# Stationary-weight units of a two-block transformer kernel: hi and lo steps paired tile by tile

## The chip, the cores and the metric

One Trainium2 chip, one core. The metric is the device time of one execution in microseconds (us). The engines are called as the profile calls them: PE (TensorE matmul), PEld (its weight loads), DVE (VectorE), ACT (ScalarE), POOL (GpSimd), SP (SyncE, which issues the weight DMAs).

## The reference, cut to what matters

The input is `x` of 256 tokens by 2048 features. It goes through two layers of a first block and one layer of a second block. Nearly all the work is dense projections of the form

```python
h = x @ w_in                      # 2048 x 6672, twice (first block)
mkv = mem @ w_mem_kv              # 2048 x 1024, twice
out = y @ w_out                   # 2048 x 2048, twice
proj = rms_norm(x) @ w_in_2       # 2048 x 11272
y_a @ w_up_a, y_b @ w_up_b        # 1024 x 2048 each
merged @ w_o                      # 2048 x 2048
h @ w_ffn_in                      # 2048 x 11264
(silu(gate) * up) @ w_ffn_down    # 5632 x 2048
```

all in fp32. Between them stand attention over bands, gated linear recurrences, memory attention, norms and gates, which are small.

## The kernel before, in words

**Precision.** Each fp32 operand is held as two fp32r numbers: hi (the rounded value) and lo (what is left of it). A product is three terms: hi times hi, hi times lo and lo times hi. `Split` (L117) keeps an activation as hi and lo side by side, so that `act.both(k)` is 512 columns (256 tokens of hi, 256 of lo) of feature tile k, and `act.hi_of(k)` the 256 hi columns alone.

**Units.** The weights come in units of 512 KB (128 partitions by 1024 columns). `plan` (L248) lists them in the order of use. For a unit, `send` (L291) issues the DMA on SP into one of NR = 5 `raw` buffers; `split` (L304) lets ACT write `wh` (a copy of `raw` rounded to fp32r) and then DVE write `wl` = `raw` - `wh`, in one of NH = 4 pairs of buffers. `cut[n]` is the pair of tokens (ACT's, DVE's) of unit n. When DVE has done unit n, SP may refill its `raw` buffer (`send(n + NR)`).

`take` (L373) gives the number of the next unit and writes the split of the unit AHEAD = 2 later into the queues of ACT and DVE. The pairs of buffers go round: `give_back` (L286) puts a pair at the end of the list `places` with the PE tokens that release it, one for `wh` and one for `wl`, and `split` takes the first of the list. So the split of unit n + 2, queued when unit n is taken, uses the pair of unit n - 2. Each engine works through its own queue in the order in which the Python program wrote it; semaphores tie them.

**Two kinds of units.**

- F units (`unit_f`, L419) give a transposed result (features by tokens). The weights are stationary: four feature tiles kk by two column tiles t. For each of these eight 128 x 128 tiles there is a hi step, whose weights are a tile of `wh` and whose moving operand is `act.both(k)` (512 columns, written to one PSUM bank), and a lo step, whose weights are the same tile of `wl` and whose moving operand is `act.hi_of(k)` (256 columns, added to columns 256 to 511 of the same bank). Tile t goes to bank `pr[t]`, so that the bank changes from one tile to the next. A step is one LDWEIGHTS and one MATMUL.
- T units (`token_steps`, L432, used in `cols_t`, `half_pass` and the last stage) have the activations stationary and 512 columns of `wh` or `wl` moving: 12 steps of 512 columns each.

`run_unit` (L403) writes first all hi steps, the first of them behind the ACT token of the unit (and other waits of the pass), then all lo steps, the first behind the DVE token. The last hi step and the last lo step each give a token, and these release `wh` and `wl`. In an F unit that is eight hi steps and then eight lo steps.

A pass (`cols_f`, L438) has two halves of four F units each (two for the 1024-row matrices); after a half, its two banks are read out by ACT and DVE (`join`, L587: ACT copies columns 256 to 511, DVE adds columns 0 to 255). Attention, recurrences, gates and norms are generators, of which a piece is written into the queues after each unit (`step_all`, `step_lane`).

The change touches `unit_f` alone. `run_unit` stays in use for T units.

Of the kernel before, what the change touches and what calls it, by code (L numbers as in the profile page):

```python
# [5 lines left out]
D, S, P = 2048, 256, 128  # L6
# [143 lines left out]
def build(nc, A, out):  # L150
# [3 lines left out]
    with ctx:  # L154
# [20 lines left out]
        def op(eng, fn, *waits):  # L175

            count[eng] += 1
            queues[eng].append((waits, fn(LATER), done[eng], 1))
            return (done[eng], count[eng])

        def mm(fn, *waits):

            queues["pe"].append((waits, fn(LATER), None, 0))
# [89 lines left out]
        sent, cut, t_const = [], [], []  # L273
# [12 lines left out]
        def give_back(n, hi_tok, lo_tok):  # L286

            if not (state["leave"] and any(place[n] is x for x in extra)):
                places.append((place[n], (hi_tok, cut[n][1]), (lo_tok,)))
# [83 lines left out]
        def take(ahead=None):  # L373

            n = state["next"]
            state["next"] += 1
            if state["ramp"]:
                state["ramp"] -= 1
                state["ahead"] += 1
            while len(cut) < min(n + (state["ahead"] if ahead is None else ahead) + 1, len(units)):  # L380
                split(len(cut))
            return n
# [15 lines left out]
        def one(fn, last, waits=()):  # L398
            if last:
                return op("pe", fn, *waits)  # L400
            mm(fn, *waits)

        def run_unit(n, hi_steps, lo_steps, waits, keep=False):  # L403


            toks = []
            for steps, w in ((hi_steps, cut[n][:1] + waits), (lo_steps, cut[n][1:])):
                for j, fn in enumerate(steps):
                    tok = one(fn, j == len(steps) - 1, w)
                    w = ()  # L410
                toks.append(tok)
            if not keep:
                give_back(n, *toks)
            return tok

        def step(o, s, m, start, stop):
            return lambda e: e.matmul(o, s, m, start=start, stop=stop, skip_group_check=True)

        def unit_f(act, pr, u, nu, waits):  # L419

            n = take()
            h, l = place[n]
            his, los = [], []
            for kk in range(4):
                k = 4 * u + kk
                for t in range(2):
                    o, c = banks[pr[t]], kk * S + t * P
                    his.append(step(o, h[:, c:c + P], act.both(k), k == 0, False))
                    los.append(step(o[:, S:2 * S], l[:, c:c + P], act.hi_of(k), False, k == 4 * nu - 1))
            return run_unit(n, his, los, waits)  # L430

        def token_steps(act, b, t, k, h, l, kk, start, stop):  # L432

# [24 lines left out]
        def cols_t(act, nk=KT, waits=(), first=0, tiles=None, pr=None, among=False, late=False):  # L458


            pr = pr or pair()
            ready = tuple(waits) + bank_free[pr[0]] + bank_free[pr[1]]
            for k0 in range(0, nk - 8 if late else nk, 2):
                if among and (k0 % 4 == 0 or among == "early" and k0 == 2):
                    among_tok.append(cut[take()])
                    ready += among_tok[-1]
                n = take()
                h, l = place[n]
                k_ = (k0 + first) % nk
                w = ready  # L470
                if tiles is not None and k_ % 4 == 0:
                    while tiles[k_ // 4] is None:
                        step_posts()
                    w += tiles[k_ // 4]
                ready = ()
                his, los = [], []
                for kk in range(2):
                    for t in range(2):
                        a, b = token_steps(act, banks[pr[t]], t, k_ + kk, h, l, kk, k0 + kk == 0, k0 + kk == nk - 1)
                        his += a  # L480
                        los += b
                tok = run_unit(n, his, los, w)
                if k0 + 2 < nk:
                    step_all()
                step_lane(0)
                step_lane(1)
            if not late:
                return pr, tok
            return pr, [take(), take(), take(0), take(0)]
# [15 lines left out]
        def cols_t_halves(made, hooks, between):  # L505


            pr = pair()
            ns = [take(0) for _ in range(4)]
            free = [bank_free[pr[t]] for t in range(2)]  # L510
            half_pass(X, pr, 0, ns, 0, True, False, True, [made[0, u // 2] + (free[0] if u == 0 else ()) for u in range(4)], hooks)
            state["ahead"], state["leave"] = AHEAD, True
            between()
            half_pass(X, pr, 1, ns, 0, True, False, False, [made[1, u // 2] + (free[1] if u == 0 else ()) for u in range(4)])
            for u in range(4, 8):
                n = take()
                his, los = [], []
                for kk in range(2):
                    for t in range(2):
                        a, b = token_steps(X, banks[pr[t]], t, 2 * u + kk, *place[n], kk, False, u == 7 and kk == 1)  # L520
                        his += a
                        los += b
                tok = run_unit(n, his, los, made[0, u // 2] + made[1, u // 2])
                step_all()
                step_lane(0)
                step_lane(1)
            state["leave"] = False
            return pr, tok
# [20 lines left out]
        def narrow_f(act, waits=()):  # L549


            pr = pair()
            n = take()
            w = cut[n] + tuple(waits) + bank_free[pr[0]]
            for k in range(KT):
                fn = lambda e: e.matmul(banks[pr[0]][0:48, :], place[n][0][:, 48 * k:48 * k + 48], act.both(k),
                                        start=k == 0, stop=k == KT - 1, skip_group_check=True)
                if k == KT - 1:
                    tok = op("pe", fn)
                else:  # L560
                    mm(fn, *w)
                w = ()
            give_back(n, tok, tok)
            return pr[0], tok
# [508 lines left out]
        for l_ in range(2):  # L1073
# [13 lines left out]
            b, tok = narrow_f(X, waits=x_ready)  # L1087
# [3 lines left out]
            def gate_sums():  # L1091
# [27 lines left out]
            pr, tok = cols_t(X)  # L1119
# [12 lines left out]
                lambda t, h, m=mv[l_]: m[:, t * 512 + h * P:t * 512 + (h + 1) * P],  # L1132
                y_tiles(yraw, 12), lambda t: S, m_ready, sm_bufs, outs, scale=SC))

            for g in range(2):
# [6 lines left out]
                pr, tok = cols_t(X)  # L1142
# [45 lines left out]
            for n in range(4):  # L1188
# [12 lines left out]
                pr, tok = cols_t(Y, first=8, tiles=tiles if n == 0 else None, among=l_ == 0 and n == 3, late=late)  # L1201
# [225 lines left out]
        for g in range(2):  # L1427
# [29 lines left out]
            if g:  # L1457
                pr, tok = cols_t(X)
# [7 lines left out]
            if g == 0:  # L1466
# [3 lines left out]
                lambda t, h, v_=v_: v_[:, t * 512 + h * P:t * 512 + (h + 1) * P], False, 1.0,  # L1470
                HNW, EPS_RMS, yraw2[:, 4 * g * S:4 * (g + 1) * S], ready, li_bufs, outs))
            if g == 0:
# [4 lines left out]
                b, tok = narrow_f(X)  # L1477
# [57 lines left out]
        for g in range(2):  # L1535
# [8 lines left out]
            pr, tok = cols_t(X)  # L1544
# [113 lines left out]
        for n in range(4):  # L1658
# [3 lines left out]
            pr, tok = cols_t(X, tiles=tiles3 if n == 0 else None, pr=pr, late=n == 3)  # L1662
# [125 lines left out]
        def ready_group(g):  # L1788
# [6 lines left out]
        pr, tok = cols_t_halves(feat.made, {  # L1795
            1: lambda: feat.turn(0, (2, 3), (6, 7), z0[2]), 2: lambda: feat.turn(1, (0, 1), (4, 5), z1[0]),
            3: lambda: feat.turn(1, (2, 3), spare, z1[1])}, between4)
# [5 lines left out]
        pr, tok = cols_t(X)  # L1803
# [36 lines left out]
        def down(k, c, n, w):  # L1840

            his, los = [], []
            for t in range(2):
                for b in range(2):
                    x, y = down_steps(k, c, t, b, n)
                    his += x
                    los += y
            return run_unit(n, his, los, w)

        for k in range(FF // P):  # L1850
# [3 lines left out]
            for c in range(2):  # L1854
                n = take()
                tok = down(k, c, n, ring[g] + ready[c])
# [8 lines left out]
        for t in range(2):  # L1865
            for c in range(2):
                for b in range(2):
                    steps = []
# [4 lines left out]
                    for i, fn in enumerate(steps):  # L1873
                        tok = one(fn, i == len(steps) - 1, w)
# [126 lines left out]
```

How the kernel before makes its waits and increments, by code:

```python
        def run(name, e):  # L1915
            seen = {}
            for waits, fn, s_, n in queues[name]:
                for s, v in waits:
                    if seen.get(s.name, 0) < v:
                        e.wait_ge(s, v)
                        seen[s.name] = v
                if fn is not None:
                    ins = fn(e)
                    if s_ is not None:
                        ins.then_inc(s_, n)
```

## Time and profile before

| | |
|---|---|
| three runs | 2424.87, 2426.34, 2426.42 us; median 2426.34 |
| the profiled execution: its own time | 2426.7 us |
| its span, from the first to the last instruction | 2424.9 us |
| PE busy | 2401.3 us (99%), 13053 matmuls |
| PEld busy | 2070.0 us (85%), 13053 loads |
| DVE busy | 1542.0 us (64%) |
| ACT busy | 1279.9 us (53%) |
| HBM traffic | 188 GB/s over the span |
| mean granted TensorE clock | 0.997 |

PE is busy when any matmul is under way. Matmuls overlap, since one lasts longer than the time to the next one's start, so a busy PE is not one that streams columns all the time. How long a step takes is read from the starts of successive steps. Columns of a timeline row are: start in us, duration in us from the first start to the last end of the merged instructions, engine, line, operation, output<-inputs by the program's names, tile and shape, and xN for N instructions merged; in brackets the idle time before it and what ended that. A LDWEIGHTS row reads `banks<-xx,wh` as its matmul does; line 83 is the helper that writes every matmul.

### The profile page before, as it was taken

Reading aid. Unit: us, or ns where it says so; the run is one execution under the profiler, and the core shown is the slowest. Engines: PE = TensorE matmul, PEld = TensorE weight load, DVE = VectorE, ACT = ScalarE, POOL = GpSimd, SP = SyncE. Lnnn points to the kernel's source line nnn. Section 1 sums busy time; section 2 is a strip of 40 time slices with the busy share of each in tenths; the row PEclk is TensorE's granted clock in tenths of the full one; section 3 lists DMA queues with packets and bytes.
Section 4 is the critical chain, followed back from the end, with each engine's and each line's share of the span. In section 5 each row is a group of like instructions: output and inputs, shape, how many; then the busy total and the mean of one; then the engine's idle time right before and its main releaser. Section 6 shows DMA issues by size and latency. Waiting matters only on the chain.

```text
span 2424.9 us, 32948 instructions
## 1 busy us (share of the span) xinstructions
PE 2401.3 (99%) x13053; PEld 2070.0 (85%) x13053; DVE 1542.0 (64%) x1755; ACT 1279.9 (53%) x1738; POOL 7.5 (0%) x14
## 2 busy tenths in 40 slices
PE   9999999999999999999999999999999999999998
PEld 7888888888888888788888888888888888888887
DVE  6575567665655677685765567766566666665555
ACT  5445466444445655565664457554655555554443
POOL 0000000000000000000000000000000000000000
PEclk9999999999999999999999999999999999999999
DMA  8544546665445664544445545575555555557553
GB/s 297 195 156 148 182 164 262 216 222 181 149 150 181 235 235 144 186 162 151 165 157 182 174 156 175 191 275 188 187 197 186 182 191 193 182 191 254 195 191 139
DMA packets 127850, 458.84 MB, mean 189 GB/s; under 512 B 13616, under 2 KB 20304, under 8 KB 124752
## 3 DMA queue, kind: packets, MB, share of 16 engines
q1 hardware_dynamic: 126736, 450.38, 53.6%
q0 software_dynamic: 816, 6.29, 0.7%
q8 instruction: 102, 1.67, 0.3%
q14 instruction: 52, 0.43, 0.1%
q10 hardware_dynamic: 144, 0.07, 0.0%
HBM read 448.30 MB, written 8.39 MB: 188 GB/s over the span
## 4 chain that ended last, share of the span: by engine, by line
PE 94%; DVE 2%; ACT 2%; DMA 1%; issue 1%; DVEq 0%; SPq 0%; ACTq 0%
PE banks L83 93%; PE banks L86 1%; ACT wh L47 1%; DVE wl L50 1%; DMA raw<-in_w_in_f 0%; ACT tb L47 0%; DMA raw<-in_kv_t 0%; DVE x_buf L59 0%; ACT sm_s L47 0%; ACT t L47 0%; DVE b L62 0%; DVE o_buf L50 0%; DVE sm_s L50 0%; DVE u L50 0%; DVE ub L50 0%
## 5 line engine op out<-in xcount | busy, mean ns | idle before, releaser
L50 DVE TENSOR_TENSOR wl<-raw,wh 128x1024 fp32r<-128x1024 f32 x776 | 937.1, 1222 | 391.1 <-ACT wh L47 389.4
L47 ACT ACTIVATE wh<-raw 128x1024 fp32r<-128x1024 f32 (+1 forms) x779 | 803.2, 1051 | 347.7 <-PE banks L83 241.0
L83 PE MATMUL banks<-xx,wh 128*128 128x512 f32 (+1 forms) x3760 | 948.8, 394 | 0.0
L83 PEld LDWEIGHTS banks<-xx,wh 128*128 128x128 f32 (+1 forms) x3760 | 674.9, 188 | 128.0 <-issue 0.7
L83 PEld LDWEIGHTS banks<-xx,wl 128*128 128x128 f32 x3712 | 506.3, 190 | 36.7
L83 PE MATMUL banks<-xx,wl 128*128 128x256 f32 x3712 | 517.4, 282 | 0.0
L83 PE MATMUL banks<-wh,xx 128*128 128x512 f32 x1504 | 376.3, 390 | 0.0
L83 PEld LDWEIGHTS banks<-wh,xx 128*128 128x128 f32 x1504 | 280.6, 188 | 57.7
L83 PE MATMUL banks<-wl,xx 128*128 128x512 f32 x752 | 203.9, 389 | 0.0
L83 PEld LDWEIGHTS banks<-wl,xx 128*128 128x128 f32 x752 | 141.2, 188 | 29.3
L83 PE MATMUL banks<-wh,yy 128*128 128x512 f32 x416 | 103.5, 390 | 1.6 <-ACT wh L47 1.6
L83 PEld LDWEIGHTS banks<-wh,yy 128*128 128x128 f32 x416 | 77.7, 188 | 18.4 <-ACT wh L47 2.4
L47 ACT ACTIVATE le<-le 128x512 f32<-128x512 f32 (+1 forms) x32 | 27.1, 846 | 90.8 <-DVE le L50 84.6
L83 PE MATMUL banks<-yy,wh 128*128 128x512 f32 x256 | 64.1, 392 | 0.0
L47 ACT ACTIVATE hraw<-banks 128x512 f32<-128x512 f32 x20 | 12.0, 598 | 87.2 <-PE banks L83 87.2
L47 ACT ACTIVATE z<-banks 128x512 f32<-128x512 f32 x24 | 14.3, 598 | 78.9 <-PE banks L83 78.9
L83 PE MATMUL banks<-wl,yy 128*128 128x512 f32 x208 | 55.9, 389 | 0.0
L50 DVE TENSOR_TENSOR hraw<-banks,hraw 128x512 f32<-128x512 f32 x20 | 13.8, 692 | 64.7 <-ACT hraw L47 64.7
L83 PEld LDWEIGHTS banks<-yy,wh 128*128 128x128 f32 x256 | 46.0, 189 | 8.2
L50 DVE TENSOR_TENSOR xl<-raw,xh 128x1024 fp32r<-128x1024 f32 x32 | 38.6, 1223 | 20.7 <-ACT xh L47 20.4
L47 ACT ACTIVATE xh<-raw 128x1024 fp32r<-128x1024 f32 x32 | 33.3, 1058 | 30.6 <-PE banks L83 16.8
L50 DVE TENSOR_TENSOR z<-banks,z 128x512 f32<-128x512 f32 x24 | 16.6, 691 | 51.4 <-ACT z L47 51.4
(234 smaller groups left out, 1881.2 us busy)
## 6 DMA issues: line engine op xcount, KB each, us to landing
raw<-in_w_in_f SPq DMA_DIRECT2D x304, 512.0 KB, 3.3
raw<-in_w_ffn_f SPq DMA_DIRECT2D x160, 512.0 KB, 3.6
raw<-in_w_ffn_down SPq DMA_DIRECT2D x88, 512.0 KB, 4.3
raw<-in_w_in_t SPq DMA_DIRECT2D x80, 512.0 KB, 3.5
raw<-in_w_out_t SPq DMA_DIRECT2D x64, 512.0 KB, 5.0
raw<-in_w_o_t SPq DMA_DIRECT2D x32, 512.0 KB, 4.5
raw<-in_kv_t SPq DMA_DIRECT2D x16, 512.0 KB, 5.3
raw<-in_kv_f SPq DMA_DIRECT2D x16, 512.0 KB, 4.2
```

The lines of the kernel that those rows point to most:

```text
L47: return lambda e: e.activation(*a, **k)
L50: return lambda e: e.tensor_tensor(*a, **k)
L83: return lambda e: e.matmul(*a, **k)
L86: return lambda e: e.transpose(*a, **k)
```

## The change

For each of the eight tiles of an F unit, the hi step is followed at once by the lo step on the same tile; then comes the next tile. The first step of the unit waits for both tokens of `cut[n]` (ACT's for `wh` and DVE's for `wl`). Only the last step of the unit gives a token, and this one token releases both `wh` and `wl`.

```diff
@@ -420,14 +420,17 @@ (unit_f)
             n = take()
             h, l = place[n]
-            his, los = [], []
+            steps = []
             for kk in range(4):
                 k = 4 * u + kk
                 for t in range(2):
                     o, c = banks[pr[t]], kk * S + t * P
-                    his.append(step(o, h[:, c:c + P], act.both(k), k == 0, False))
-                    los.append(step(o[:, S:2 * S], l[:, c:c + P], act.hi_of(k), False, k == 4 * nu - 1))
-            return run_unit(n, his, los, waits)
+                    steps.append(step(o, h[:, c:c + P], act.both(k), k == 0, False))
+                    steps.append(step(o[:, S:2 * S], l[:, c:c + P], act.hi_of(k), False, k == 4 * nu - 1))
+            for j, fn in enumerate(steps):
+                tok = one(fn, j == len(steps) - 1, cut[n] + waits if j == 0 else ())
+            give_back(n, tok, tok)
+            return tok
```

The number of steps, their operands, their sizes and the order of units stay as they are.

## Rows read from the trace of the kernel before

**Rows 1.** Busy time by engine, and the chain that ended last by engine (page).
```profile
PE 2401.3 (99%) x13053; PEld 2070.0 (85%) x13053; DVE 1542.0 (64%) x1755; ACT 1279.9 (53%) x1738; POOL 7.5 (0%) x14
...
PE 94%; DVE 2%; ACT 2%; DMA 1%; issue 1%; DVEq 0%; SPq 0%; ACTq 0%
```

**Rows 2.** PE's steps by kind, with counts (groups by form).
```profile
L83 PE MATMUL banks<-xx,wl 128*128 128x256 f32 x3712 | 517.4, 282 | 0.0
L83 PE MATMUL banks<-yy,wl 128*128 128x256 f32 x256 | 35.7, 282 | 0.0
L83 PE MATMUL banks<-mem,wl 128*128 128x256 f32 x128 | 17.8, 282 | 0.0
```

**Rows 3.** Timeline, PE: the start of an F unit, and of the 45th after it.
```profile
1465.34 2.00 PE L83 MATMUL banks<-xx,wh 128*128 128x512 f32 x8
...
1591.04 1.32 PE L83 MATMUL banks<-yy,wh 128*128 128x512 f32 x5
```

**Rows 4.** Timeline, PE: F units following one another.
```profile
1802.60 2.00 PE L83 MATMUL banks<-xx,wh 128*128 128x512 f32 x8
1804.44 1.11 PE L83 MATMUL banks<-xx,wl 128*128 128x256 f32 x8
1805.39 2.00 PE L83 MATMUL banks<-xx,wh 128*128 128x512 f32 x8
```

**Rows 5.** Timeline, PEld: single loads around the two switches of those units.
```profile
1801.65 0.19 PEld L83 LDWEIGHTS banks<-xx,wl 128*128 128x128 f32 x1
1801.76 0.19 PEld L83 LDWEIGHTS banks<-xx,wl 128*128 128x128 f32 x1
...
1802.60 0.19 PEld L83 LDWEIGHTS banks<-xx,wh 128*128 128x128 f32 x1
1802.83 0.19 PEld L83 LDWEIGHTS banks<-xx,wh 128*128 128x128 f32 x1
1803.07 0.19 PEld L83 LDWEIGHTS banks<-xx,wh 128*128 128x128 f32 x1
...
1803.76 0.19 PEld L83 LDWEIGHTS banks<-xx,wh 128*128 128x128 f32 x1
...
1808.18 0.19 PEld L83 LDWEIGHTS banks<-xx,wh 128*128 128x128 f32 x1
1808.42 0.19 PEld L83 LDWEIGHTS banks<-xx,wh 128*128 128x128 f32 x1
```

**Rows 6.** Timeline, PE: the F unit behind a run of T steps.
```profile
102.83 1.98 PE L83 MATMUL banks<-xx,wh 128*128 128x512 f32 x8
104.64 1.12 PE L83 MATMUL banks<-xx,wl 128*128 128x256 f32 x8
```

**Rows 7.** Timeline, PEld: two 256-column matmuls onto the same columns of a bank.
```profile
1438.59 0.19 PEld L83 LDWEIGHTS banks<-negative,ident_r 128*128 128x128 f32 x1
1438.71 0.19 PEld L83 LDWEIGHTS banks<-xx,wh 128*128 128x128 f32 x1
```

**Rows 8.** Waits of PE, the largest group (releaser: us in total, times, longest).
```profile
PE banks L83 <- DVE lqe L50: 7.3, 3, 5.2
```

**Rows 9.** Timeline, DVE and PE: a lo split that ends after its unit began.
```profile
33.22 1.23 DVE L50 TENSOR_TENSOR wl<-raw,wh 128x1024 fp32r<-128x1024 f32 x1 [0.89 <-ACT wh L47]
34.21 2.00 PE L83 MATMUL banks<-mem,wh 128*128 128x512 f32 x8
...
1005.92 1.22 DVE L50 TENSOR_TENSOR wl<-raw,wh 128x1024 fp32r<-128x1024 f32 x1
1006.23 2.00 PE L83 MATMUL banks<-xx,wh 128*128 128x512 f32 x8
```

**Rows 10.** Timeline, PE: behind the last such unit.
```profile
1029.28 2.04 PE L83 MATMUL banks<-lqe,lke 128*128 128x128 f32 x8 [5.25 <-DVE lqe L50]
```

**Rows 11.** Timeline, PE and ACT: a release of `wh` and the split that follows.
```profile
2045.62 2.00 PE L83 MATMUL banks<-xx,wh 128*128 128x512 f32 x8
2047.70 1.06 ACT L47 ACTIVATE wh<-raw 128x1024 fp32r<-128x1024 f32 x1 [1.24 <-issue]
```

## The prediction

> **What bounds the kernel now.** I read the chain of work that ended last first: 94% of it is PE [rows 1]. PE is busy for 2401.3 of 2424.9 us, so that all its gaps together are 23.6 us [rows 1], and the largest group of its waits, for `lqe`, has 7.3 us in three waits [rows 8]. So the kernel ends when PE has gone through its steps, and what counts is the time from one step's start to the next. The groups by form give the number of steps with lo weights, one for each pair that the change reorders: 3712 + 256 + 128 = 4096, in 512 F units of eight pairs [rows 2].
>
> The price of a pair today: between two starts of F units 45 apart lie 1591.04 - 1465.34 = 125.70 us [rows 3], 2.793 us a unit, 349.1 ns a pair. Inside a unit the eight hi steps take 1.84 us (1802.60 to 1804.44), 230 ns each, and the eight lo steps 0.95 us, 119 ns each [rows 4]. 4096 pairs at 349.1 ns are 1430 us, 59% of the span. So one nanosecond per pair is worth 4.1 us. The whole question is whether a hi and a lo step side by side cost more or less than 349.1 ns.
>
> Single weight loads say what a step costs by its place [rows 5]. A load starts as the matmul before it starts, so their distances are those of the steps. Among the lo steps, the first after hi steps takes 0.11 us (1801.65 to 1801.76), and the other seven 0.84 together (1801.76 to 1802.60), 120 ns each; with 0.953 for all eight (2.793 less 1.84) the first has 113 ns. Among the hi steps, the first takes 0.23 (1802.60 to 1802.83; 0.24 in another unit, from 1808.18), the second 0.24, and the first five 1.16 together, 232 ns each; the last three of a unit are left with 1804.44 - 1803.76 = 0.68, 227 ns each [rows 4, 5]. A unit that comes behind 512-column steps of a T run has its eight hi steps in 104.64 - 102.83 = 1.81 us, 226 ns each [rows 6], where eight take 1.84 behind lo steps. So a settled hi step costs 227 ns, and after lo steps it takes about five hi steps, some 27 ns in all, to settle. The first lo step is cheap (113 ns), each lo step behind a lo step costs 120.
>
> **The change, part by part.**
>
> *The order of steps.* Nothing is added or removed on PE: 16 loads and 16 matmuls a unit before and after. Every lo step becomes a first lo step, and every hi step a first hi step. The trace never has the two kinds in turn, so the price must be bounded. A lo step lies between 113 ns (the first after hi) and 120 (in a run); it is nearest to the first kind, since a 512-column step stands ahead of it: 113. A hi step lies between 227 (settled) and 236 (the second after a switch, where the row's 0.24 is read at its lower side); it is nearest to the first hi step behind a lo step, 0.23 to 0.24: 233.3. The pair is 346.6 to 346.7 ns, 2.4 less than today. 4096 x 2.4 ns = 9.8 us. The two ends are 227 + 113 = 340 (-37 us) and 236 + 120 = 356 (+28 us).
>
> *What of it reaches the end.* Of the chain 94% is PE [rows 1]. Where PE waits for another engine, what it saves ahead of the wait is lost. I take 9.8 x 0.94 = 9.2 us.
>
> *The bank.* The lo step adds to the columns that the hi step ahead of it has just written, where today the bank alternates from step to step. The nearest row: two 256-column matmuls that add to the same columns of one bank, 0.12 us apart, the price of any lo step [rows 7]. In the change the distance at those columns is the same, since the hi step writes them in its second half. Cost nothing; if it isn't so, it shows as a pair above 349 ns, like the third rival.
>
> *The wait at the unit's start.* Today lo weights may be ready 1.84 us after the start. DVE finishes the lo split of most units well ahead. In six units it ends after the unit has begun, for instance at 33.22 + 1.23 = 34.45 against 34.21, and at 1005.92 + 1.22 = 1007.14 against 1006.23 [rows 9]. The other overshoots are of the same size or smaller, and the six sum to 2.7 us. Four of the six lie between 1006 and 1021 us, ahead of the idle 5.25 us in which PE waits for the chain of DVE that makes `lqe` [rows 10], and vanish in it. The two at 34 and 45 us cost 0.24 and 0.21 us and some 0.1 us each for the load that waits with them. Queued behind the waiting step are the unit's other steps and nothing of other work. I take +0.6 us; the bound is 0 below and 3 above.
>
> *The later release of `wh`.* The token of the last hi step, 0.95 us ahead of the unit's end, goes. ACT does use it: the hi steps of the unit at 2045.62 end at 2047.62, and the next split starts at 2047.70 [rows 11]. It will start about 0.9 us later. That split is for the unit four further on, which starts at 2045.62 + 4 x 2.79 = 2056.8. Split and lo split take 1.06 + 1.23 us and would end at about 2051, with 6 us to spare. What ACT has queued behind the split are pieces of attention and gates that depend on PE work behind later units, and the DMA that refills `raw`, also 0.9 us later, has over four units. Cost nothing; with the cover gone (where ACT and DVE are the chain, 4% of it [rows 1]) at most 0.9 us at each of three waits for `lqe` [rows 8], +3 us. One token less per unit on PE: nothing to be seen.
>
> *Sum.* The profiled execution took 2426.7 us, its span is 2424.9. 2426.7 - 9.2 + 0.6 = 2418.1. The median of the runs is 0.4 below the profiled one, so 2417.7; I say 2418.
>
> **The rivals.** About 0.2% (5 us) is what a measurement of this kernel can tell from no change.
>
> *Settled pairs: 2392 us.* The five slow hi steps may be a matter of leaving a run of lo steps, and with hi and lo in turn PE may never leave its settled state. Then the pair is 340 ns: 9.1 x 4096 = 37 us, 35 of them on the chain, +0.6. For it: each load has a longer step to hide beside half of the time, and 113 and 227 are exactly in the ratio of the columns. Against it: it is the lo steps that put the hi steps out of their settled state, and in the change every hi step stands behind one.
>
> *No difference: 2427 us.* The cheap first lo step may be borrowed from the hi steps, and given back. If the alternation stays unsettled, a hi step costs 232 or 233 and a lo step 116 to 117: 349. For it: the first lo step is 7 ns cheaper than the others, and the first hi step 6 dearer than a settled one, which nearly cancels. A page would put it here by another way. The Trainium skill, "TensorE: Matmul & The Clock Gate", sections "LDWEIGHTS (loading the stationary operand)" and "Back-to-back issue gap", gives a load of 128 columns 107 ns and a warm step its columns over 2.4 GHz plus 2.5 ns, 216 and 109; the load then fits beside either step, so the order would not matter. The trace doesn't agree on the size (227 and 113 to 120).
>
> *The load beside the short step: 2443 us.* Each hi tile's weights can only be loaded while the 256-column lo step runs. If a lo step between two hi steps is held by that load as those of a run are, it costs 120 ns, and the hi step behind it 233: 353.3 ns, +4.2 x 4096 x 0.94 = +16.2, +0.6. It decides for slower from about 350.3 ns a pair on. For it: today's last lo step, behind which a hi tile is loaded, takes 0.12 as well. Against it: the first lo step after hi takes 0.11 although the load beside it is as long. With 236 for the hi step it would be 2454.
>
> **How the numbers follow.** Forecast (a gain between 5 and 20 us) 0.42; settled 0.14; no difference 0.22; load beside the short step 0.22, half of it above 2434. The prediction is 2418. The range reaches down over the settled case (2390) and up over no difference with the 3 us waits and the lower half of the slower case (2434). Faster by over 0.2%: 0.42 + 0.14 = 0.56. Within 0.2%: 0.22. Slower: 0.22.
>
> **What would show it.** In the profile after: PE rows of 16 steps no longer in eights; starts of F units 2.77 us apart in place of 2.793 (2.72 in the settled case, 2.83 in the slower one); loads alternately 0.23 and 0.11 apart; T units unchanged at 227 ns a step; the waits for `lqe` within 1 us of before; a first-step wait for `wl` near 34 and 45 us of a few tenths. I am wrong if the unit's period moves by less than 0.01 us or upward, or if PE's waits grow by more than 3 us.

## The result, and the profile after

The changed kernel takes 2434.59 us (median of 6 runs, 2433.78 to 2435.97) against 2425.99 for the kernel before on the same chip; the ratio is 1.0038, 95% interval [1.0025, 1.0051]. It is 8.6 us slower. The forecast was 8 us faster, and the measured time lies just above the range.

The page of the changed kernel, engines and the chain that ended last, which answer to [rows 1]:

```profile
PE 2408.4 (99%) x13053; PEld 2059.8 (85%) x13053; DVE 1543.5 (63%) x1755; ACT 1286.6 (53%) x1738; POOL 7.5 (0%) x14
...
PE 93%; DVE 3%; ACT 2%; DMA 1%; issue 1%; SPq 0%; DVEq 0%; ACTq 0%
```

The same number of steps on PE, the same chain. The span grew from 2424.9 to 2434.2 us. Two terms can carry that: the steps and the waits. Waits first, to [rows 8] (releaser: us in total, times, longest):

```profile
PE banks L83 <- ACT wh L47: 5.9, 8, 1.2
PE banks L83 <- DVE lqe L50: 5.8, 3, 4.0
PE banks L83 <- DVE wl L50: 1.3, 3, 0.9
```

The wait for `wl` is new (1.3 us), the one for `lqe` is 1.5 us shorter, the one for `wh` has grown. That is not 9 us. The steps: the timeline of PE in the ffn stage, where the starts of successive rows are the starts of successive steps, answers to [rows 4, 5]:

```profile
1800.11 0.40 PE L83 MATMUL banks<-xx,wh 128*128 128x512 f32 x1
1800.34 0.28 PE L83 MATMUL banks<-xx,wl 128*128 128x256 f32 x1
1800.46 0.40 PE L83 MATMUL banks<-xx,wh 128*128 128x512 f32 x1
1800.69 0.28 PE L83 MATMUL banks<-xx,wl 128*128 128x256 f32 x1
1800.81 0.40 PE L83 MATMUL banks<-xx,wh 128*128 128x512 f32 x1
1801.05 0.28 PE L83 MATMUL banks<-xx,wl 128*128 128x256 f32 x1
1801.17 0.40 PE L83 MATMUL banks<-xx,wh 128*128 128x512 f32 x1
```

From 1800.11 to 1801.17 are three pairs in 1.06 us: 353 ns a pair, the hi steps 0.23, 0.23 and 0.24, the lo steps 0.12, 0.12 and 0.12. Another stretch of the same kernel, the merge of the two mixers:

```profile
1519.90 0.39 PE L83 MATMUL banks<-yy,wh 128*128 128x512 f32 x1
1520.13 0.27 PE L83 MATMUL banks<-yy,wl 128*128 128x256 f32 x1
1520.24 0.40 PE L83 MATMUL banks<-yy,wh 128*128 128x512 f32 x1
1520.47 0.28 PE L83 MATMUL banks<-yy,wl 128*128 128x256 f32 x1
1520.59 0.39 PE L83 MATMUL banks<-yy,wh 128*128 128x512 f32 x1
1520.82 0.27 PE L83 MATMUL banks<-yy,wl 128*128 128x256 f32 x1
1520.93 0.40 PE L83 MATMUL banks<-yy,wh 128*128 128x512 f32 x1
```

Here three pairs take 1.03 us. Over longer stretches, between a unit's start and that of the 45th unit after it in the merge stage, and of the 154th in the ffn stage:

```profile
1469.98 0.39 PE L83 MATMUL banks<-xx,wh 128*128 128x512 f32 x1
...
1594.78 0.39 PE L83 MATMUL banks<-yy,wh 128*128 128x512 f32 x1
...
1747.81 0.40 PE L83 MATMUL banks<-xx,wh 128*128 128x512 f32 x1
...
2183.11 0.40 PE L83 MATMUL banks<-xx,wh 128*128 128x512 f32 x1
```

124.80 / 45 = 2.773 us a unit, 346.7 ns a pair, and 435.30 / 154 = 2.827 us, 353.3 ns. The kernel before had 2.793 in both [rows 3, 4]. So the new order has two rhythms, one cheaper and one dearer than eight and eight. Taking the steps of each unit behind its first eight, every one of the 512 F units is clearly in one of the two: 199 at 346.7, 313 at 353.3. In 411 places one such unit follows another with nothing between them; the rhythm changes in one of them, behind a stop of PE of 0.94 us (at 1011.89). In steps that is 313 x 8 x 4.2 ns - 199 x 8 x 2.4 ns = +6.7 us.

The two traces, summed from start to start, give the same: all steps that read `wh` or `wl` as weights take 1450.6 us before and 1457.3 after. The stops of PE (the time beyond a step's usual distance) cost 3.1 us more: 0.65 at the two starts that wait for `wl` near 33 and 45 us, 3.3 at waits of T units for `wh` near 395 and 865 us, less 0.8 elsewhere. The other steps take 0.8 us less. In the profiled execution before, the granted clock was 0.69 from 10 to 14 us, behind PE stops of 1.1 and 2.0 us: seven T steps there lie 427 ns apart in place of 227 (some 1.5 us), which the changed kernel's trace hasn't. Together with 0.2 us at the end this makes up the 9.3 us between the two spans.

### The profile page after: what moved, and what is told of

It is laid out like the page before. It is cut to its first block, busy times and chain, and to the rows that moved or that the text cites. A ratio compares the mean times of both kernels' runs of the same rounds, so it can differ in the third digit from the quotient of the medians.

```text
span 2434.2 us, 33355 instructions
## 1 busy us (share of the span) xinstructions
PE 2408.4 (99%) x13053; PEld 2059.8 (85%) x13053; DVE 1543.5 (63%) x1755; ACT 1286.6 (53%) x1738; POOL 7.5 (0%) x14
## 4 chain that ended last, share of the span: by engine, by line
PE 93%; DVE 3%; ACT 2%; DMA 1%; issue 1%; SPq 0%; DVEq 0%; ACTq 0%
PE banks L83 92%; PE banks L86 1%; DVE wl L50 1%; ACT wh L47 1%; DMA raw<-in_w_in_f 1%; ACT tb L47 0%; DMA raw<-in_kv_t 0%; ACT t L47 0%; DVE x_buf L59 0%; ACT sm_s L47 0%; DVE b L62 0%; DVE ub L50 0%; DVE o_buf L50 0%; DVE le L50 0%; DVE sm_s L50 0%
## 5 line engine op out<-in xcount | busy, mean ns | idle before, releaser
L83 PE MATMUL banks<-xx,wh 128*128 128x512 f32 (+1 forms) x3760 | 1326.5, 399 | 0.9 <-DVE wl L50 0.9
L83 PE MATMUL banks<-xx,wl 128*128 128x256 f32 x3712 | 1039.1, 280 | 0.0
L83 PEld LDWEIGHTS banks<-xx,wh 128*128 128x128 f32 (+1 forms) x3760 | 703.2, 187 | 173.9 <-ACT t L47 1.2
L83 PEld LDWEIGHTS banks<-xx,wl 128*128 128x128 f32 x3712 | 700.8, 189 | 0.8
L83 PE MATMUL banks<-wh,xx 128*128 128x512 f32 x1504 | 376.4, 390 | 0.0
L83 PE MATMUL banks<-yy,wh 128*128 128x512 f32 x256 | 88.8, 394 | 0.0
L83 PE MATMUL banks<-yy,wl 128*128 128x256 f32 x256 | 70.9, 277 | 0.0
```

Source lines behind the costliest of these rows:

```text
L83: return lambda e: e.matmul(*a, **k)
```

## The experiments

The theories: **A**, the order of long and short steps costs, and waits do little; **B**, the joint wait and the late release cost; **C**, the lo step is held by the bank that the hi step ahead of it writes; **D**, a rhythm is caught where PE enters a run of pairs, and kept; **E**, the stage sets the rhythm by its traffic or addresses. Ratios are to the kernel before, run on the same chip in turn.

### Eight and eight with the new waits

```diff
-            return run_unit(n, his, los, waits)
+            steps = his + los
+            for j, fn in enumerate(steps):
+                tok = one(fn, j == 15, cut[n] + waits if j == 0 else ())
+            give_back(n, tok, tok)
+            return tok
```

> The steps stay eight hi and eight lo; the unit waits for both splits at its start and gives one token at its end, as in the changed kernel. Theory A (the order of the steps costs, the waits and the later release do little): units stay 2.793 us apart, and the time is 1 to 2.5 us above the kernel before, with PE's waits up by that much (near 34, 45, 385 and 940 us). Theory B (the later release and the joint wait are what costs): the time is 7 to 9 us above the kernel before.

2428.05 us against 2425.68: +2.4, ratio 1.0012 [1.0003, 1.0021], which is 0.7 to 5.1 us. The waits are a real term, at the upper end of theory A's sum, and by the medians less than a third of the loss. B, which asked for 7 to 9 us, falls as the main cause.

### Pairs with the release and the lo wait of before

The first step waits for `cut[n][:1]`, the second for `cut[n][1:]`; steps 15 and 16 give a token each.

> Hi and lo in turn as in the changed kernel, but the first lo step alone waits for the lo split, and the last hi step gives the token that releases wh. Only one step lies between the two, so that the release is about as late as in the changed kernel, but the lo wait is off the first step. Theory A: pairs of 346.7 ns in some stretches and 353.3 in others as in the changed kernel, the time 6.5 to 8.5 us above the kernel before, up to 1 us less than the changed kernel. Theory B: the time falls back by 1 us or more towards the kernel before, as far as the wait for wl was the cost.

2433.24 us, ratio 1.0028 [1.0017, 1.004]. The two rhythms are there nearly as in the changed kernel, with 315 of 512 units at the dear one. Against its own runs of the kernel before it is +7.6 us, the changed kernel +8.6; the intervals overlap, so that this difference is as expected, but not shown.

### The lo step one tile behind

```diff
+            steps = [his[0]] + [s for i in range(7) for s in (his[i + 1], los[i])] + [los[7]]
```

> Waits and token as in the changed kernel; the lo step of a tile comes after the hi step of the next tile (h0 h1 l0 h2 l1 ... h7 l6 l7), so hi and lo still take turns, but no step adds to the bank that the step ahead of it has just written. Theory C (the lo step is held by the bank that the hi step ahead of it writes): the dear pairs of 353 ns vanish everywhere, units 2.77 us or less apart, the time 5 to 12 us below the changed kernel's 2434.6. Theory A (the turn of long and short steps is what costs, whatever the bank): 350 to 353 ns a pair inside such units, units 2.78 to 2.83 us apart, the time within 4 us of the changed kernel.

2436.89 us, ratio 1.0047 [1.0035, 1.006]. The timeline of PE in its ffn stage:

```profile
1825.67 0.28 PE L83 MATMUL banks<-xx,wl 128*128 128x256 f32 x1
1825.79 0.39 PE L83 MATMUL banks<-xx,wh 128*128 128x512 f32 x1
1826.01 0.28 PE L83 MATMUL banks<-xx,wl 128*128 128x256 f32 x1
1826.13 0.40 PE L83 MATMUL banks<-xx,wh 128*128 128x512 f32 x1
1826.37 0.28 PE L83 MATMUL banks<-xx,wl 128*128 128x256 f32 x1
...
1827.08 0.28 PE L83 MATMUL banks<-xx,wl 128*128 128x256 f32 x1
```

The lo step now stands behind a hi step that writes the other bank, and from 1826.01 to 1827.08 three pairs still take 1.07 us. So C falls. The expectation says more than the edit does: tiles take the two banks in turn, so that in h1 l0 h2 the steps l0 and h2 write the same bank, and half of the neighbours are still such pairs. That the bank doesn't part the two prices follows from the pairs themselves, which write the banks in the same order at 346.7 and at 353.3 ns. The twos below, where the bank changes at every step, cost 348.3, between them; a small cost of the bank within both is not excluded. With this order the unit takes 2.820 us in the ffn stage and in the merge stage alike, where the changed kernel had 2.827 and 2.773. That speaks against E too.

### Twos

```diff
+            steps = [s for i in range(0, 8, 2) for s in (his[i], his[i + 1], los[i], los[i + 1])]
```

> Waits and token as in the changed kernel, order h0 h1 l0 l1 h2 h3 l2 l3 and so on, with the bank changing from step to step as in the kernel before. Theory A: a switch from lo to hi costs the hi steps some 5 to 9 ns each and a switch from hi to lo gives 7 back, so two tiles cost 233 + 236 + 113 + 119 = 701 ns, 350.5 a pair, units 2.80 us apart: 5 to 7 us above the kernel before. Theory C: no bank is written twice in a row, so it costs 347 ns a pair or less, at or below the kernel before but for 1 to 2.5 us of waits.

2425.99 us, ratio 1.0001 [0.9992, 1.001]: better than theory A's number. With the 2.4 us of waits that this kernel also carries, its steps must be some 2 us cheaper than eight and eight; summed in its trace they are 2.5 us cheaper. So the twos were run again with separate waits.

### Twos and fours with separate waits

`cut[n][1:]` is awaited at the first lo step, and the last hi step gives the token for `wh`.

> Order h0 h1 l0 l1 h2 h3 l2 l3 and so on, with the lo split awaited at the first lo step and wh released by the last hi step. Units stay at 2.787 us as measured for the twos with joint waits, 3 us less than eight and eight in all. If the joint wait costs what the eight and eight with joint waits showed (2.4 us), nearly all of it comes back only as far as it is the wait at the start and not the later release: 2424 to 2425.5, 0 to 2 us below the kernel before.

2421.85 us against 2424.72, ratio 0.9988 [0.9979, 0.9997]: 2.9 us faster than the kernel before. The timeline of PE:

```profile
1820.29 0.62 PE L83 MATMUL banks<-xx,wh 128*128 128x512 f32 x2
1820.75 0.40 PE L83 MATMUL banks<-xx,wl 128*128 128x256 f32 x2
1820.99 0.63 PE L83 MATMUL banks<-xx,wh 128*128 128x512 f32 x2
1821.46 0.39 PE L83 MATMUL banks<-xx,wl 128*128 128x256 f32 x2
1821.68 0.63 PE L83 MATMUL banks<-xx,wh 128*128 128x512 f32 x2
```

Four pairs in 1821.68 - 1820.29 = 1.39 us, 348 ns a pair. Over 154 units of the ffn stage and 45 of the merge stage a unit takes 2.787 us, 348.3 ns a pair: no second rhythm was seen.

> Order h0 to h3, l0 to l3, h4 to h7, l4 to l7, waits as in the twos with split tokens. If a switch from lo to hi costs what the first four hi steps behind lo steps show (233 + 236 + 228 + 233), and the four lo steps 113 + 3 x 120, a group of four is 1403 ns, 350.7 a pair, 2.806 us a unit: 6 to 8 us above the kernel before. If there is a gain in any grouping smaller than eight, it is below the kernel before.

2428.91 us, ratio 1.0017 [1.0008, 1.0026], +4.2; units are 2.807 us apart over 154 units, as the sum of single steps said. The time was somewhat less than expected (4.2 us in place of 6 to 8, interval 1.9 to 6.3). From eight over four and two to one the pair costs 349.1, 350.8, 348.3 and 346.7 or 353.3 ns: there is no trend in the number of switches.

### Disturbing the rhythm

The changed kernel with a dictionary of F-unit numbers, whose first unit of a half pass gets for instance (d) one pair turned round, (c) hi hi lo lo at its start, (g) one fp32 transpose ahead of it that the first hi step overwrites, or nothing.

> The changed kernel; in the ffn stage (160 F units, all at 2.827 us in the changed kernel) the first unit of each half pass gets one of eight disturbances in a mixed order: eight and eight, twos, hi hi lo lo at the start, one pair turned round, all pairs but two turned round, one small fp32r or fp32 matmul ahead that is overwritten, four and four at the start; or none. The three units behind it stay plain. Theory D (a rhythm of 346.7 or 353.3 ns a pair is caught at the entry into a run of pairs, and kept): some disturbances bring the plain units behind them to 2.773 us and some to 2.827, and where the first unit has none, the units keep what the half pass before it had. Theory E (the stage sets it, by the traffic of ACT, DVE and the DMAs or the addresses): all plain units stay at 2.827.

One execution, 2430.7 us. Three stretches of plain units, cut at unit starts (us, PE busy and steps, PEld, DVE, ACT, POOL, clock, DMA share, GB/s):

```profile
1754.10:1765.19 11.09, 11.09 (x66) 9.78 (x65) 8.07 (x9) 7.31 (x10) 0.00 (x0) 1.00 0.60 194
1843.92:1855.22 11.30, 11.30 (x67) 9.80 (x65) 8.07 (x9) 7.32 (x10) 0.00 (x0) 1.00 0.42 138
1888.94:1911.13 22.19, 22.19 (x130) 19.40 (x129) 14.08 (x15) 11.93 (x15) 0.00 (x0) 1.00 0.57 189
```

The first four units, behind a half pass whose first unit had one pair turned round, take 2.773 us each; the second four take 2.82, and the last eight, two half passes with nothing changed in them, 2.774. All are in the stage that in the changed kernel has 2.827 throughout, with the same work on DVE and ACT. The plain units behind a disturbance were at 2.773 in some half passes and at 2.827 in the others, and undisturbed half passes kept what they found. The plain units behind it were cheap in four of five places for the fp32 transpose and in five of six for hi hi lo lo at the start, but in one of four for one pair turned round, and in none of five for eight and eight. What PE was in before matters too: behind dear units, the fp32 transpose and hi hi lo lo led to the cheap rhythm in seven of seven places, behind cheap ones in two of four. The average rhythm isn't all of it: four and four at the start, in four places behind dear units, gave cheap twice and dear twice. Nine of the places fall into four groups with the same disturbance and the same distances of the four steps ahead, within 1 ns; in each group the outcome is the same. That is a hint that the place in the repeating pattern counts, from one execution, and no proof. E falls, D holds.

### One pair turned round

The edit, without the table of disturbances (it has this one entry):

```diff
+            if fno == 356:                  # first unit of the long run of the ffn stage
+                steps = steps[:4] + [los[2], his[2]] + steps[6:]
```

> The changed kernel with two of its 8192 F steps exchanged: in the first unit of the long unbroken run of the ffn stage (156 F units from 1745 us on), the third pair is lo, hi in place of hi, lo. Theory D (the rhythm is caught at the entry and kept): the run goes over to pairs of 346.7 ns and stays there to its end, units 2.773 us apart in place of 2.827; 156 x 0.0535 = 8.3 us less than the changed kernel's 2434.6, so 2426. Theory E (the stage sets it): within 1 us of 2434.6.

2426.03 us against 2424.37, ratio 1.0012 [1.0002, 1.0021]. That is 8.6 us below the changed kernel's median, and 6.9 when each is taken against its own runs of the kernel before, for two steps exchanged among 8192. The turned pair in the timeline of PE (the two rows x2), and unit starts 154 apart:

```profile
1744.19 0.40 PE L83 MATMUL banks<-xx,wh 128*128 128x512 f32 x1
1744.42 0.40 PE L83 MATMUL banks<-xx,wl 128*128 128x256 f32 x2
1744.66 0.63 PE L83 MATMUL banks<-xx,wh 128*128 128x512 f32 x2
...
1746.64 0.39 PE L83 MATMUL banks<-xx,wh 128*128 128x512 f32 x1
...
2173.74 0.39 PE L83 MATMUL banks<-xx,wh 128*128 128x512 f32 x1
```

427.10 / 154 = 2.773 us, where the changed kernel took 435.30 us for the same units: 8.2 us in this run alone. Nine of its eleven runs lie between 2424.5 and 2427.4, two at 2432.7 and 2435.0. In the profiled execution 145 units ahead of the ffn stage are dear (153 in the changed kernel) and so are the stage's first four, but none of the 156 from the exchange on. The two slower runs are where the dear rhythm would put them, but they have no profile, so that the entry was missed in them is a guess.

### The twos, and the cheap rhythm where it holds

Twos with separate waits for the first 305 F units, pairs from there on, with the one pair turned at unit 356.

> Twos with split tokens as measured (2421.9) for the first 305 F units; hi and lo in turn from there on, where one stretch (47 units) held 346.7 ns a pair in the changed kernel and the ffn stage (160 units) gets the one pair turned round at unit 356. Theory D: 2.773 us a unit in both, 207 x 0.014 = 2.9 us less than the twos alone: 2419, 6 to 7 us below the kernel before. If the entry is met in another phase because the units ahead are twos, the ffn stage runs at 2.827 and the time is 2428.

2419.72 us against 2424.37, ratio 0.9981 [0.9973, 0.999]: 4.6 us faster than the kernel before, the lowest ratio of the versions here; its interval overlaps that of the twos alone, so that the step from 2.9 to 4.6 us is not shown by the times. The ffn run is at 2.773 us a unit, and its eleven runs lie within 2418.8 to 2421.0.

### The two waits apart

Both with eight and eight. In the first, `cut[n]` is awaited at the start and the last hi step still gives the token for `wh`; in the second, the waits are as before, and one token releases both.

> Eight and eight; the unit waits for both splits at its start, but the last hi step still gives the token that releases wh. The two parts together cost 2.4 us. If it is the joint wait: 1.5 to 2.5 us above the kernel before. If it is the later release: within 1 us of it. My forecast put the joint wait at 0.6.

> Eight and eight; the first lo step alone waits for the lo split, but one token at the unit's end releases both wh and wl. If the later release is what costs, by splits and weight DMAs that start 0.9 us later where the stage has no slack: 1.5 to 2.5 us above the kernel before, with longer waits of PE for wh near 385 and 940 us. My forecast put it at nothing.

The joint wait alone: 2427.69 against 2424.60, ratio 1.0012 [1.0003, 1.0021]. The late release alone: 2425.74, ratio 1.0003 [0.9994, 1.0012], not to be told from none. The two intervals overlap (0.7 to 5.1 us and -1.5 to 2.9), and the traces decide: against the kernel before, PE's stops cost 2.2 us more with the joint wait and nothing more with the late release. The wait is the cost. Timeline of PE with the joint wait:

```profile
30.82 1.98 PE L83 MATMUL banks<-mem,wh 128*128 128x512 f32 x8
32.63 1.11 PE L83 MATMUL banks<-mem,wl 128*128 128x256 f32 x8
33.97 2.07 PE L83 MATMUL banks<-mem,wh 128*128 128x512 f32 x8 [0.23 <-DVE wl L50]
...
37.22 2.08 PE L83 MATMUL banks<-mem,wh 128*128 128x512 f32 x8 [0.23 <-ACT wh L47]
...
46.03 2.08 PE L83 MATMUL banks<-mem,wh 128*128 128x512 f32 x8 [0.20 <-DVE wl L50]
...
398.44 1.88 PE L83 MATMUL banks<-wh,yy 128*128 128x512 f32 x7 [1.18 <-ACT wh L47]
```

The unit at 33.97 starts 1.34 us after the lo steps of the one ahead, in place of 0.95 [rows 4]: the idle 0.23 costs 0.39 us. The missing 0.16 is a matter of the view: it counts idle time from the end of the last lo step, whose row is 0.28 us long where the next step would have started after 0.12. There are three such stops instead of my two. The wait for `wh` in a run of T units at 398 was 0.62 us before (start at 396.88 there) and is 1.18 now. The stop of 0.90 us that appears at 1009.60 is absorbed by the wait for `lqe`, as forecast: the longest one falls from 5.2 to 4.1 us.

## Why the prediction was wrong

**What held.** PE's steps set the time; T units stayed as they were (their 1504 largest-group hi steps keep PE busy for 376.4 us, 376.3 before); no cost of two steps on one bank is to be seen (pairs at 346.7 ns against twos, which never do it, at 348.3); of the four overshoots near 1006 to 1021 us one stop came (0.90 to 0.94 us), and it vanishes in the wait for `lqe`; the later release of `wh` is not measurable with eight and eight. 346.7 ns a pair is the price in 199 of 512 units. But it isn't made up as forecast, of 233 + 113 each time: the starts, read to 1 ns, repeat 231 + 112 and 233 + 117 in the merge stage, and 230 + 117 throughout the ffn stage of the kernel with one pair turned. That the number came out to 0.1 ns is luck.

**The step that failed** is *The order of steps*: "every lo step becomes a first lo step, and every hi step a first hi step", one price for all 4096 pairs. It took the first intervals after a switch as the price of a steady alternation. The alternation has two prices, and the third rival's 353.3 is the other: 313 units run at it. That rival had the number, by luck as well: it took 233 + 120 for every pair, and the dear rhythm repeats 236 + 113, 233 + 117 and 241 + 120, three pairs in 1060 ns. The cause it gave, the load of the next hi tile beside the short step, was not tested by itself, and the same load stands beside the same step at 346.7 ns. In place of the forecast -9.8 the steps cost +6.7 us, and all of it reached the end: the factor 0.94 had nothing to take off.

**The second term** was mis-sized: *The wait at the unit's start* had +0.6 us and measured +2.4 with the release, +3.1 alone. I counted the overshoot and 0.1 us for the load, 0.34 and 0.31 us for two stops; a short stop costs 0.36 to 0.40 us and there are three in the first 60 us, 1.1 us. The larger part was left out: T units wait longer for `wh` near 397 and 860 us (0.6 us more at each, start against start). In the changed kernel the same two places cost 3.3 us more than before, and PE's stops 3.1 us in all. What makes ACT's splits later there was not tested apart. 6.7 for the steps, 3.1 for the stops, less 0.8 in the other steps (with the slow clock at the start of the trace before) and 0.2 at the end make 9.2, against 9.3 between the spans; the medians differ by 8.6.

**The chances.** The rivals each took one price for the whole kernel. Two prices could not be read in the trace of before, but a warning could: hi steps behind a switch took 0.23, 0.24 and about 0.23 us before they settled at 227 ns [rows 5], so that a step's price depends on more than the step ahead of it, and the first price behind a switch need not be that of a steady alternation. The slower side deserved more than 0.22.

What stays open: what inside PE makes two rhythms, what of the entry picks one, and why two runs of the one-pair kernel missed. In the changed kernel's trace entries behind the 512-column steps of T units led to the dear rhythm each time (11 of 11), those behind short fp32 matmuls to either. Why T units near 395 and 865 us wait longer in the changed kernel is open too.

## What to carry to other kernels

Where the order of unequal matmuls changes, don't price the new order by the first steps after a switch: measure the period over tens of units, in each stage, since the same instructions can run in two rhythms (here 2% apart) that last for hundreds of microseconds. Moving a wait from the middle of a unit to its start can cost more than the overshoot it uncovers, here by longer waits further on. And a grouping that repeats without two rhythms (twos, 348.3 ns) is worth more than one whose best case is better and whose mean is not.

## What the runs showed of the hardware that was not expected

- A run of alternating 512- and 256-column fp32r steps, each with its own 128-column load, keeps one of two periods, 346.7 or 353.3 ns a pair, across at least 155 units (some 430 us) at a granted clock of 1.00 in both. Read to 1 ns, the dear one is a pattern of three pairs (236 + 113, 233 + 117, 241 + 120), the cheap one of two (231 + 112, 233 + 117) or of one (230 + 117).
- Exchanging two neighbouring steps at the entry moves a whole run from one to the other: 2.827 to 2.773 us a unit in the profiled execution, and by their times in nine of eleven runs.
- A step's price depends on the grouping and not on the number of switches: 350.8 ns a pair for fours, 349.1 for eights, 348.3 for twos.
- By the load time and the warm gap of a single matmul that the Trainium skill, "TensorE: Matmul & The Clock Gate", gives in its sections "LDWEIGHTS (loading the stationary operand)" and "Back-to-back issue gap", as the prediction read them, the order would not matter. The runs don't agree: 346.7 to 353.3 ns a pair by order and entry.
- A stop of PE that the view puts at 0.20 to 0.23 us adds 0.36 to 0.40 us from start to start, since it is counted from the end of a row of 0.28 us behind which the next step usually starts after 0.12.
